# A three-stage mixture-of-experts block on one core: whole-matrix weight transfers, five units outside the ring, and another order of the rotary swaps

## The reference

```python
h = x
for i in range(2):
    mix = diff_attention(h, ...) if i == 0 else pool_mixer(h, ...)
    h = layer_norm(ALPHA * h + mix, ln_g[i, 0], ln_b[i, 0])
    ffn = hier_moe(h, ...)                 # 32 experts, D_EXPERT = 512, top 2
    h = layer_norm(ALPHA * h + ffn, ln_g[i, 1], ln_b[i, 1])
# second block: rmsnorm, forgetting attention beside an RG-LRU, then
# rmsnorm and a mixture of 32 experts of width 256, then the final rmsnorm

def run_block(xb, e):                      # for the tokens routed to expert e
    h = silu(xb @ w_gate[e]) * (xb @ w_up[e])
    return h @ w_down[e]

def apply_partial_rope(t, cos, sin):       # first 16 of 64 dims of q and k
    r1, r2, rest = t[..., :8], t[..., 8:16], t[..., 16:]
    return concatenate([r1 * c - r2 * s, r1 * s + r2 * c, rest], axis=-1)
```

## Time and profile before

| | us |
|---|---|
| median of 3 runs | 2048.75 (2044.33 to 2049.82) |
| the profiled execution's own time | 2049.75 |
| its span, first to last instruction | 2047.9 |
| PE busy | 1923.4 (94%) |
| DVE, ACT, POOL busy | 672.8, 403.5, 152.2 |
| attention, first chunk to head | 68 to 279 |
| first mixture, pair 0 to last down | 337.2 to 809.5 |
| second mixture, pair 0 to last down | 978.8 to 1450.6 |

### The profile page before, as it was taken

One profiled execution on the slowest core, in us unless ns is written; L12 is line 12 of the kernel. 1 busy time (PEld: TensorE's weight loads), 2 busy tenths in 40 slices (PEclk: granted clock), 3 DMA queues, 4 the chain that ended last, 5 costly groups with the idle time before them and its releaser, 6 DMA issues.

```text
span 2047.9 us, 24899 instructions
## 1 busy us (share of the span) xinstructions
PE 1923.4 (94%) x9773; PEld 1037.1 (51%) x9773; DVE 672.8 (33%) x1621; ACT 403.5 (20%) x866; POOL 152.2 (7%) x208
## 2 busy tenths in 40 slices
PE   8899999999999998999999999999799999998877
PEld 4355556455545544746545544545454444765543
DVE  0156665311111112636221111111639323631214
ACT  1044432111011011111111111011224222121222
POOL 0111101000000000000100000000010001211100
PEclk9999999999999999999999999999899999999999
DMA  9711107999999998813899999999941211799995
GB/s 335 221 48 49 45 25 269 419 420 421 420 420 421 420 420 355 293 54 108 361 419 421 420 421 421 420 419 418 333 142 47 77 42 35 284 387 419 420 419 213
DMA packets 127281, 598.97 MB, mean 292 GB/s; under 512 B 17545, under 2 KB 46105, under 8 KB 64223
## 3 DMA queue, kind: packets, MB, share of 16 engines
q1 hardware_dynamic: 111567, 568.06, 69.5%
q0 software_dynamic: 15632, 29.79, 4.3%
HBM read 575.58 MB, written 37.03 MB: 299 GB/s over the span
## 4 chain that ended last, share of the span: by engine, by line
PE 63%; DMA 26%; DVE 6%; ACT 2%; issue 2%; SPq 0%; POOL 0%; DVEq 0%; ACTq 0%; POOLq 0%
DMA ring<-in_moe_w_up_dram 19%; PE bank L1033 18%; PE bank L685 8%; PE bank L1068 7%; PE bank L942 6%; DMA ring<-in_w_up_dram 5%; PE bank L838 5%; PE bank L699 3%; PE bank L671 3%; PE bank L1207 1%; PE bank L787 1%; PE bank L1168 1%; PE bank L1184 1%; PE bank L718 1%; PE bank L748 1%
## 5 line engine op out<-in xcount | busy, mean ns | idle before, releaser
L1033 PE MATMUL bank<-ring,work 128*64 128x512 f32 (+1 forms) x2976 | 565.4, 536 | 46.2 <-DMA ring<-in_moe_w_up_dram 24.6
L1033 PEld LDWEIGHTS bank<-ring,work 128*64 128x64 f32 x2976 | 231.2, 140 | 376.5 <-issue 352.7
L1799 DVE TENSOR_TENSOR work<-work,bank 64x512 f32<-64x512 f32 (+1 forms) x96 | 86.7, 904 | 790.4 <-ACT work L1355 790.4
L1068 PE MATMUL bank<-ring,work 128*64 128x512 f32 x1280 | 286.9, 599 | 6.3 <-DVE work L1917 6.3
L942 PEld LDWEIGHTS bank<-work 128*128 128x128 f32 x2048 | 233.6, 192 | 26.0 <-issue 25.9
L942 PE MATMUL bank<-work 128*128 128x128 f32 x2048 | 242.7, 277 | 0.0
L685 PE MATMUL bank<-hT,ring 128*128 128x512 f32 x512 | 235.7, 602 | 0.7 <-ACT work L1270 0.7
L1068 PEld LDWEIGHTS bank<-ring,work 128*64 128x64 f32 x1280 | 90.0, 137 | 168.7 <-issue 160.7
L1355 ACT ACTIVATE work<-bank 64x512 f32<-64x512 f32 (+1 forms) x96 | 50.0, 521 | 526.4 <-PE bank L1033 526.4
L1366 ACT ACTIVATE work<-bank 64x512 f32<-64x512 f32 x96 | 56.7, 590 | 490.4 <-PE bank L1068 490.4
L685 PEld LDWEIGHTS bank<-hT,ring 128*128 128x128 f32 x512 | 93.2, 193 | 104.8 <-issue 102.9
(11 more groups left out here) (311 smaller groups left out, 1587.4 us busy)
## 6 DMA issues: line engine op xcount, KB each, us to landing
ring<-in_moe_w_down_dram SPq DMA_DIRECT2D x128, 1024.0 KB, 19.4
ring<-in_moe_w_gate_dram SPq DMA_DIRECT2D x126, 1024.0 KB, 20.7
ring<-in_moe_w_up_dram SPq DMA_DIRECT2D x126, 1024.0 KB, 22.7
ring<-in_w_down_dram SPq DMA_DIRECT2D x32, 1024.0 KB, 25.5
ring<-in_w_gate_dram SPq DMA_DIRECT2D x30, 1024.0 KB, 22.0
ring<-in_w_up_dram SPq DMA_DIRECT2D x30, 1024.0 KB, 24.1
ring<-in_attn_w_qkv_dram SPq DMA_DIRECT2D x12, 1024.0 KB, 12.4
work<-y_rows SPq DMA_DIRECT2D x12, 1024.0 KB, 9.6
```

Source lines behind the costliest of these rows:

```text
L1033: mm = pe.matmul(GU2[of_pair][(gate_rows, up_rows)[a][of_pair], 0:F], xgT[pair % 2][:, per * kk + k, BLK * of_pair:BLK * of_pair + BLK], v ...
L1068: mm = pe.matmul(DN2[par][BLK * n:BLK * n + BLK, :], hT_[:, 2 * kk + k, BLK * par:BLK * par + BLK], v[:, k, 512 * n:512 * n + 512], start= ...
L1799: dve.tensor_tensor(dealt(hg_pair[own_rows[par], 0:F], F // P), as_dealt(sg_pair[own_rows[par], 0:F], F // P), as_dealt(GU2[par][up_rows[p ...
```

## The change

Four things are edited. (1) In the first two mixtures a whole matrix (two ring units side by side, 128 rows of 16 KB) is loaded by one transfer where two transfers of rows of 8 KB stood, in the order gate, up of each expert; SP waits until both places are free, and PE frees the four gate and up units of an expert together, after 32 matmuls. (2) Five units of the last two experts stand outside the ring instead of two: gate of expert 30 in `h`, the first half of its up in two gaps of `work`, gate of expert 31 in `hT`. The last pair has seven ring units. (3) So that `h` is free, the four copies of the residual move from the mixture's head to ACT's part of the last pair, and the loads of `y_rows` wait for them. (4) The chunks of a pair of heads are made in the order query, key, query, key; the scores wait for two `rope`s for each head, and the swaps of the first eight chunks alternate between two tiles.

```diff
-SPARE = 2
+SPARES = (5, 5, 4)
...
+                def load_spares():
+
+                    sp.wait_ge(tiles_written, turns[HEADS[l][1]].src_all)
+                    sp.dma_start(spare_gate[0], matrices(l, E - 2)[0]).then_inc(spare_loaded, 16)
                     sp.wait_ge(routing.logits, T * (l + 1))
...
+                    for n in range(2):
+                        sp.dma_start(gaps[n], matrices(l, E - 2)[1][:, D * n:D * n + D]).then_inc(spare_loaded, 16)
+                    sp.dma_start(spare_gate[1], matrices(l, E - 1)[0]).then_inc(spare_loaded, 16)
...
+                def load_matrix(i, v, src):
+
+                    u = m.base + v
...
+                    sp.wait_ge(units_used, u - UNITS + 2 + TURN * m.upb * i)
+                    sp.dma_start(places[:, UW * (u % UNITS):UW * (u % UNITS) + 2 * UW], src)\
+                        .then_inc(unit_loaded[u % UNITS], 16)
+                    sp.sem_inc(unit_loaded[u % UNITS + 1], 16)
...
+                if l < 2:
+                    sp.wait_ge(routing.scaled, T * l + tiles[-1] + 1)
...
-                return first["qk"] + 2 * pair + n // 2, n % 2
+                return first["qk"] + 2 * pair + n % 2, n // 2
...
-                    pe.wait_ge(at.rope, 4 * (hh // 2) + 3 + hh % 2)
+                    pe.wait_ge(at.rope, 2 * hh + 2)
...
+                    if at_unit:
+                        mm.then_inc(main.used, len(at_unit))
...
+                    if last_pair(i, q) and l < 2:
+                        residual(0)
+                        residual(1)
                     product(i, 2 * q + 1)
+                    if last_pair(i, q) and l < 2:
+                        residual(2)
+                        residual(3)
...
-                if cc:
-                    pool.wait_ge(at.rope, cc)
+                if cc > 1:
+                    pool.wait_ge(at.rope, cc if cc > SWAPS else cc - 1)
```

More of the change, by code:

```diff
@@ L112, in program @@
         hT = sb("hT", [P, K, S])
-        ring = [sb(f"ring{i}", [P, UW]) for i in range(UNITS)]
+        places = sb("ring", [P, UNITS * UW])
+        ring = [places[:, UW * i:UW * i + UW] for i in range(UNITS)]
         work = sb("work", [P, 18432])
@@ L509, in load, with matrices @@
                 sp.dma_start(ring[u % UNITS][:, :], units[u]).then_inc(unit_loaded[u % UNITS], 16)
[L511 to L523, removed]
+            def matrices(l, e):
+                return [a[e].rearrange("(p k) n -> p (k n)", p=P) for a in experts[l]]
@@ L536, in load_scraps @@
                 def load_scraps():
-                    gate, up, _ = list(expert_units(m, l, E - 2))
+                    sp.wait_ge(routing.logits, T * (l + 1))
+                    for a in range(2):
+                        sp.dma_start(spare[a].rearrange("p a n -> p (a n)"), matrices(l, E - 1)[a])\
+                            .then_inc(spare_loaded, 16)
+                    gate, up, _ = matrices(l, E - 2)
                     sp.wait_ge(tiles_written, turns[HEADS[l][1]].src_all)
-                    sp.dma_start(spare_up, up).then_inc(spare_loaded, 16)
+                    sp.dma_start(lnp, up).then_inc(spare_loaded, 16)
@@ L562, in pair @@
-                    if nth_pair(i, q) == (1 if l == 2 else 0):
-                        load_spare()
-                        if l == 2:
-                            load_scraps()
+                        source, at_unit = matrices(l, TURN * i + s), gate_up_units(m, i, s)
+                        for a in range(2):
+                            if m.F == 512 and (a, 0) in at_unit:
+                                load_matrix(i, at_unit[a, 0], source[a])
+                            elif m.F == 512 and (a, 1) in at_unit:
+                                load(i, at_unit[a, 1], halves(source[a])[1])
+                            elif (a, 0) in at_unit:
+                                load(i, at_unit[a, 0], source[a])
@@ new lines, in pair @@
+                    for s in (2 * q, 2 * q + 1):
+                        source = matrices(l, TURN * i + s)[2]
+                        if m.F == 512:
+                            load_matrix(i, down_unit(m, i, s), source)
+                        else:
+                            load(i, down_unit(m, i, s), source)
+                    if nth_pair(i, q) == 0 and l < 2:
+                        load_spares()
+                    if nth_pair(i, q) == 1 and l == 2:
+                        load_scraps()
@@ L576, in mixture @@
                         sp.wait_ge(m.ov.used, m.upb * j + 1)
-                        for q, src in enumerate(expert_units(m, l, e)):
+                        parts = [half for a in matrices(l, e) for half in (halves(a) if m.F == 512 else [a])]
+                        for q, src in enumerate(parts):
                             u = m.base + q
@@ L1543, in tile_normal, with tile_rms @@
                 dve.wait_ge(done, count0 + 2 * tt + 2)
[L1545 removed]
+            def tile_rms(l, tt, gain, dst, done):
                 r = rstd2[:, tt:tt + 1]
```

145 lines of the change are left out of this document (75 added, 70 removed).

## The result

| | before | after |
|---|---|---|
| median of 5 runs, us | 2048.75 | 2060.51 (2057.6 to 2064.98) |
| the profiled execution's own time, us | 2049.75 | 2057.91 |
| first chunk to the mixture's head, us | 210.96 | 215.55 |
| first mixture, first matmul to last down, us | 472.25 | 474.59 |
| second mixture, same | 471.77 | 472.14 |

The ratio is 1.0063, with a 95% interval from 1.0043 to 1.0083: the change makes the kernel 12 us slower. That is outside the range from 2032 to 2056, and on the side to which I gave 0.13.

A forecast was written before the change was run, and what follows sets the result against it. Bound: the mixtures' chain of waits, PE first, then DMA, the last `w_up` wait deciding. 2049.75 - 0.7 (mixtures) - 3.2 (attention) = 2045.85; 1.0 less for the median gives 2044.85, rounded 2045. Range of 8 in 10: 2032 to 2056.

The forecast's parts named there:

- What bounds the kernel: Both large mixtures: PE first, then DMA at 420 GB/s; the last wait for a `w_up` unit decides.
- the 8.81 of the last downs: Last pair of the first mixture: 8.81 against 7.11 read as a wait for units, 1.7 us to be gained.
- The unit's time: Mixture loads: rows of 16 KB save 37 ns a unit, over 164 units 6.1 us a mixture.
- The first end: Start of each mixture: four units freed together at 344.33, not two at 340.90, delay every later unit by 3.4 us.
- The second end: End of each mixture: 32 matmuls instead of 16 follow the last `w_up` landing, costing 3.2 us.
- The sum of the mixtures: Both large mixtures: first -1.2 us, second +0.5, together -0.7.
- The ring: Mixtures: SP's coarser waits for the 12 places cost nothing beyond the two ends.
- the five units: Units outside the ring: cost 0; gain only the 1.7 us in the first mixture's downs, 0 in the second.
- the residual: Four copies moved from the mixture's head to ACT's part of the last pair: nothing gained, cost 0.
- The attention's later swaps: Swaps of chunks 8, 12 and 16 beside 2 MB loads: 1.0 us each, +2.5 in all; bounds 0 to 3.0 each.
- The attention's start: First scores follow the fourth chunk at once, the next eight matmuls start earlier: net gain 5.7 us, between 4.4 and 7.4.
- The rival on the slower side: Mixtures: coarse freeing costs 6.6 us each and the stream is no faster, time 2057; chance 0.15.

The follow-up runs named there:

- before again: The kernel before the change, profiled and timed again with no edit; ratio 1.0003 to before.
- rows of 8 KB: Changed kernel with every matrix loaded by two 1 MB transfers in rows of 8 KB, PE still freeing four units together; ratio 1.0045 to before.
- fine ends: Changed kernel with gate and up of pairs 0 and 14 in both mixtures loaded by 1 MB in the old order, freed by twos; ratio 0.9978 to before.
- the split ups: Changed kernel with pair 0 by 1 MB, its attention loads held back, and only up by halves in pairs 12 to 14; ratio 0.9978 to before.
- after with late loads: Changed kernel with SP holding each 2 MB attention load until the rope of the pair of heads' last chunk is done; ratio 1.0001 to before.
- mixtures alone: Changed kernel with the attention's edits (chunk order, two swap tiles, waits for ropes) taken back; ratio 1.0060 to before.
- the bursts: Kernel before the change with the two 1 MB attention loads of a pair of heads issued together, in rows of 8 KB; ratio 1.0047 to before.
- two outside: Changed kernel with two units outside the ring instead of five and the residual's copies back in the mixture's head; ratio 1.0065 to before.

## Why the prediction was wrong

**What bounds the kernel.** Right for the mixtures: the last wait for `w_up` decides. Wrong in one reading: the 8.81 of the last downs. I took it for a wait for units and took 1.7 off. It is the clock. In 11 of the 28 mixtures profiled here they take 8.7 to 8.8, in kernels of every kind and with ten or seven ring units in the pair, in the others 7.1. The granted clock would have told it ahead: in the trace of before it is 0.80 from 801 to 809, and 1.00 in the second mixture from 1444 to 1450. I had read only the chain's length.

**The unit's time.** Right in size: 427 against 426 GB/s. Wrong in what it multiplies. The last wait moved by 3.8 us, from the mean of 8 KB rows with coarse grain (429.3) to that of 16 KB rows (425.5), where I had 6.1. The later pairs give all that was forecast: the waits stand 30.3 us apart with rows of 16 KB (152.8 to 425.6 in nine pairs, first mixture after) and 30.8 with rows of 8 KB (182.2 to 428.4 in eight, before again), 0.5 / 12 = 40 ns a unit for the 37 that I took. What is missing is missing early: the wait near 152 us stands no sooner with rows of 16 KB (152.8 and 152.5, after) than with rows of 8 KB and the same freeing (151.8 and 151.6). The cause stays open. A ring that PE hasn't freed is not it, since the engines are full there in both kernels: share 1.01 at 426 GB/s from 349 to 489 (after), share 1.01 at 420 from 342 to 482 (rows of 8 KB).

**The first end.** Forecast +3.4, measured +0.5: the last wait stands at 428.8 in the mean of the five profiles with 8 KB and fine grain, at 429.3 with 8 KB and coarse grain. With fine ends the first refill is issued 3.7 to 4.0 us into the mixture instead of 7.1, and the wait of pair 13 comes only 0.4 and 1.2 us earlier. There the rows show where the start is lost again. SP issues the last gate or up of pair 1 at 347.07 and the next load, a whole down that waits for two free places, only at 358.42; nearly all that was issued has moved by then, and the engines run partly empty. SP's timeline and the stretches with fine ends, and the same stretch of after:

```profile
347.07 0.33 SPq L572 DMA_DIRECT2D ring<-in_moe_w_up_dram  x1
358.42 3.76 SPq L572 DMA_DIRECT2D ring<-in_moe_w_down_dram  x2
```

```profile
353.00:363.00 10.00, 10.00 (x57) 4.45 (x57) 4.79 (x17) 2.31 (x4) 0.00 (x0) 1.00 0.91 354
363.00:373.00 10.00, 10.00 (x50) 3.38 (x48) 1.63 (x3) 0.65 (x2) 0.00 (x0) 1.00 0.99 392
```

```profile
359.00:369.00 10.00, 10.00 (x54) 4.21 (x54) 4.80 (x17) 2.37 (x4) 0.00 (x0) 1.00 1.02 433
```

Against 427 GB/s the two stretches lack 1.1 MB, which is 2.5 us of the 3.4. With rows of 8 KB the engines are full from the first refills on with either freeing (share 1.01 to 1.02), and why 3.4 us at the start are 0.5 at the end stays open.

**The second end.** Forecast +3.2. It is there (7.09 us behind the last landing instead of 3.65), but one fine pair can't take it back: PE reaches the last 16 matmuls of pair 14 32.2 us after the last landing of pair 13, and the landings are 30.3 apart. This was first seen in the fine ends and then used for the split ups, whose own expectation failed at another point.

**The sum of the mixtures** came out right by luck, from terms that were not: last downs at 464.3 in the mean of the kernels with the old mixtures, at 464.5 with the new, +0.2 each, where +0.5 was forecast without the clock's 1.7. The measured terms are -3.8, +0.5 and +3.4.

**The ring, the five units, the residual.** Right, all at nothing. The residual's two pairs of copies lie clear of the second silu and of the results:

```profile
795.01 3.91 ACT L1401 ACTIVATE h<-work 128x1024 f32<-128x1024 f32 x2
801.38 0.59 ACT L1385 ACTIVATE work<-bank 64x512 f32<-64x512 f32 x1 [2.45 <-PE bank L1066]
801.99 3.83 ACT L1401 ACTIVATE h<-work 128x1024 f32<-128x1024 f32 x2
809.94 0.59 ACT L1396 ACTIVATE work<-bank 64x512 f32<-64x512 f32 x1 [4.13 <-PE bank L1101]
```

**The attention's later swaps: the step that failed.** I took 1.0 us each, from a row in which a 1 MB load cost PE 0.54, and put the upper bound of 3.0 each into the range only. They cost 2.93, 2.43 and 2.38 of idle time, each nearly the upper bound, and clock behind the last; waits of over 2 us at these chunks are what I had named as a sign of being wrong. The fourth swap, which I had priced as landing with the end of its load at 102.2 to 103.5, landed at 103.9; PE waited 4.50 there, not 2 to 3. (The terms that I gave there add up to 107.1 to 108.4 for the next eight matmuls and not to 107.5 to 108.8; the turn of the weights between them, 0.44, stands in no term. They started at 109.44.)

The four waits are 12.2 us. Taking the load away from beside the swap takes the loss away (after with late loads), making it smaller takes half of the waits away (fine ends, 6.0 us), and putting it there makes the loss (mixtures alone, the bursts).

The Trainium skill ("DMA: Bandwidth & Descriptors", section "Queues, rings and completion order") says that the increment that reports a transfer's end lands only after all earlier writes of that engine, across its queues. It spoke for the upper bound, and the times agree with it: the last of the four small transfers lands 5.0 to 6.5 us after its issue, and 1.8 in quiet, where 2 MB take 4.9 at 427 GB/s. But the packets show more than a late report: the swap's own rows hadn't begun to move 3.8 us after the first issue. I had named that rule and gone by the milder row.

**The attention's start: the other half.** The gain of 5.7 was worked out against 6.5 us of idle time in one execution. Another execution of the same kernel has 1.5, and no slow matmuls behind it. The gain came in the trace (the scores stand right behind the chunk of 95.0), but with quiet swaps on both sides the new order is worth 2.1. So the attention is not -3.2 but, against before again, about +12: the waits of 13.2 against 2.0 + 1.5 give +9.7, and the slower clock behind the first and the last of them (eight matmuls in 4.75 and 4.84 for 3.60) another 2.4. The first chunk stood 3.4 us later in before again than in after, so counted from the first instruction the difference is +8.6; against the first profile it is +3.9. The +12 of the whole time is the median's, over many runs; the split of it between stages rests on single profiles.

The rival on the slower side (coarse grain costs, 2057) was near in time by luck and wrong in mechanism: the mixtures are no slower.

## What to carry to other kernels

When a change makes a transfer larger, look not only at the stage that it serves but at the stage in which it is issued: small transfers on the critical path land behind whatever stands ahead of them, and PE waits for them. Holding a prefetch back behind the small transfer costs one wait on its queue and took away the whole loss here. And a gain that is read from an idle time wants a second profile of the same kernel: the wait behind DMA landings ahead of the first scores moved by 5 us between two executions.

## What the runs showed of the hardware

- The last of four small transfers of 8 rows of 2 KB stands in the chain with 1.76 us in quiet, 2.3 to 4.4 beside a load of 1 MB issued up to 3.5 us ahead, and 4.9 to 6.8 beside 2 MB (after, mixtures alone, two outside, the bursts). Beside 2 MB none of their packets had moved 3.6 us after the first issue, where in quiet all had. Whether the 2 MB are one transfer of 16 KB rows or two of 8 KB makes little difference (attention 215.6 to 218.9 against 213.4).
- Rows of 16 KB move 425 to 427 GB/s inside the mixtures, in all eight kernels that have them, where rows of 8 KB move 420 in the other six.
- PE's clock of 1.2 GHz comes and goes in the same code: the last 32 downs of a mixture, behind idle times of 1.19 and 0.78 us, took 7.1 in 17 of 28 cases and 8.8 in 11. The idle times ahead were the same in both.
